# The opening of a transformer trunk as a stream by chunk: the first modulation computed slice by slice, its scale on TensorE and its shift on VectorE

## The reference

```python
cond = jax.nn.silu(c)
for i in range(DEPTH):
    mod = (cond @ mod_w[i] + mod_b[i])[:, None, :]
    shift1, scale1, gate1, shift2, scale2, gate2 = jnp.split(mod, 6, axis=-1)
    h = rms_norm(x, norm1_gain[i]) * (1 + scale1) + shift1
    y = swa_sink_attention(h, ...)          # layer 0; layer 1: gmlp_spatial_gating
    x = x + gate1 * y
    h = rms_norm(x, norm2_gain[i]) * (1 + scale2) + shift2
    x = x + gate2 * squared_relu_mlp(h, mlp_w1[i], mlp_w2[i])
```

## Time and profile before

| | |
|---|---|
| device time, median of 3 runs | 2563.44 us (2560.73 to 2566.36) |
| span of the profiled execution | 2568.1 us |
| TensorE busy in the span | 2438.0 us (95%) |
| VectorE busy | 1059.8 us (41%) |
| ScalarE busy | 650.8 us (25%) |
| GpSimd busy | 506.9 us (20%) |
| transfers | 189.01 MB, mean 74 GB/s |
| mean granted TensorE clock | 0.975 |

### The profile page before, as it was taken

How to read it: one execution, slowest core, us unless ns; L and a number is a source line. 1 busy time by engine, 2 the same in 40 slices (tenths; PEclk the granted TensorE clock), 3 DMA queues, 4 the chain that set the end, 5 groups by cost and what they waited for, 6 DMA issues and landing times.

```text
span 2568.1 us, 28722 instructions
## 1 busy us (share of the span) xinstructions
PE 2438.0 (95%) x10592; PEld 1942.8 (76%) x10592; DVE 1059.8 (41%) x1190; ACT 650.8 (25%) x719; POOL 506.9 (20%) x232
## 2 busy tenths in 40 slices
PE   3997889899999999998999999999899999999999
PEld 2776458688888888887788788788678888888887
DVE  7655965633333333334432442343522323232232
ACT  3322531321221221212322331122331221221221
POOL 1111221112212212211211112112122221222121
PEclk9887989899999999999999999999899999999999
DMA  6342131121221221221244221221011111111112
GB/s 240 107 140 68 37 150 41 64 84 49 75 80 49 83 72 52 87 66 41 98 127 143 89 74 41 73 82 49 25 49 50 49 41 50 49 47 43 49 49 82
DMA packets 70592, 189.01 MB, mean 74 GB/s; under 512 B 23440, under 2 KB 25360, under 8 KB 70032
## 3 DMA queue, kind: packets, MB, share of 16 engines
q1 hardware_dynamic: 52144, 127.64, 15.4%
q10 hardware_dynamic: 18400, 60.69, 6.8%
HBM read 170.48 MB, written 16.78 MB: 73 GB/s over the span
## 4 chain that ended last, share of the span: by engine, by line
issue 65%; PE 27%; POOL 7%; POOLq 0%; DVE 0%; ACT 0%; DVEq 0%
PE pp L1034 27%; POOL w_lo L267 7%; POOL pr L279 1%; POOLq L287 0%; POOLq L266 0%; DVE x L921 0%; POOLq L283 0%; DVE mod_t L624 0%; ACT tmp L307 0%; POOLq L273 0%; POOLq L278 0%; POOL kf L270 0%; POOLq L267 0%; POOL vt L271 0%; DVEq L921 0%
## 5 line engine op out<-in xcount | busy, mean ns | idle before, releaser
L267 POOL TENSOR_TENSOR w_lo<-w_raw,w_hi 128x1024 fp32r<-128x1024 f32 x194 | 473.2, 2439 | 1942.4 <-ACT w_hi L298 1942.4
L1034 PE MATMUL pp<-h_hi,w_hi 128*128 128x512 f32 x1824 | 605.7, 408 | 35.1 <-DVE h_lo L715 23.3
L1034 PE MATMUL pp<-h_lo,w_hi 128*128 128x512 f32 x1824 | 595.2, 402 | 0.0
L1034 PE MATMUL pp<-h_hi,w_lo 128*128 128x512 f32 x1824 | 593.7, 401 | 0.0
L298 ACT ACTIVATE w_hi<-w_raw 128x1024 fp32r<-128x1024 f32 x194 | 205.0, 1057 | 959.6 <-PE pp L1034 916.9
L1034 PEld LDWEIGHTS pp<-h_hi,w_hi 128*128 128x128 f32 x1824 | 346.6, 192 | 129.3 <-issue 22.4
L1034 PEld LDWEIGHTS pp<-h_lo,w_hi 128*128 128x128 f32 x1824 | 350.5, 192 | 85.3 <-issue 1.0
L1034 PEld LDWEIGHTS pp<-h_hi,w_lo 128*128 128x128 f32 x1824 | 349.6, 192 | 85.7
L1034 PE MATMUL pp<-hid_hi,w_hi 128*128 128x512 f32 x1280 | 410.4, 398 | 0.0
L1034 PE MATMUL pp<-hid_hi,w_lo 128*128 128x512 f32 x1280 | 409.0, 397 | 0.0
L1034 PE MATMUL pp<-hid_lo,w_hi 128*128 128x512 f32 x1280 | 408.9, 397 | 0.0
(11 more groups left out here) (133 smaller groups left out, 1225.0 us busy)
## 6 DMA issues: line engine op xcount, KB each, us to landing
w_raw<-weights SPq DMA_DIRECT2D x194, 512.0 KB, 3.3
mod_t<-mod_w ACTq DMA_DIRECT2D x64, 512.0 KB, 3.4
mod_first<-mod_w SPq DMA_DIRECT2D x16, 512.0 KB, 15.5
mod_late<-mod_w ACTq DMA_DIRECT2D x2, 4096.0 KB, 19.3
v_dram<-v_out ACTq DMA_DIRECT2D x16, 512.0 KB, 5.5
vf<-v_dram ACTq DMA_DIRECT2D x16, 512.0 KB, 4.4
x<-x_in SPq DMA_DIRECT2D x4, 1024.0 KB, 9.1
qf<-q_dram SPq DMA_DIRECT2D x32, 128.0 KB, 2.5
```

The source lines that it names most:

```text
L267: nc.gpsimd.tensor_tensor(out=w_lo[:, s, :, :], in0=w_raw[:, s, :, :], in1=w_hi[:, s, :, :].bitcast(f32), op=ALU.subtract).then_inc(lo_don ...
L1034: last = T.matmul(pp[s][:, cs], w[:, s, k, :], r[:, k, cs], start=(k == 0 and w is w_hi and r is hi), stop=(k == KC - 1 and w is w_lo))
```

## The change

The five small loads move from SP's queue to ScalarE's, so that x is the first thing SP loads, and the positions are staged in `sin` instead of `qa`. `mod_first` shrinks from sixteen whole tiles to four slots of 1 MB; a load now brings, for one output chunk k, the 128 outputs of both shift and scale from all eight input chunks. Slots are used again once both users are done with them.

The shift of chunk k is accumulated on VectorE in `shift_rows(k)`: eight operations of 128 x 128 in place of a share of eight operations of 128 x 1024. The scale of chunk k is eight matmuls on TensorE, with the weight block as the stationary operand and one column of `cond` moving; one more matmul sums the shift accumulator. VectorE adds bias and gain to one column at a time. h follows chunk by chunk, and the two units of the first pair follow h, with the modulation of chunk k+2 ahead of the products of chunk k on TensorE.

```diff
             for i in range(4):
                 sp.dma_start(x[:, 2 * i:2 * i + 2, :], x_in[:, 2 * i:2 * i + 2, :]).then_inc(x_ld[i], 16)
-            for q in range(2 * KC):
-                if q == KC:
+            for k in range(KC):
+                if k == 3:
                     for s in range(2):
                         sp.dma_start(w_raw[:, s, :, :], weights[s]).then_inc(raw_in[s], 16)
-                sp.dma_start(mod_first[:, q, :], mod_w[q]).then_inc(mf_in[q], 16)
+                if k >= 4:
+                    sp.wait_ge(sh_acc, k - 3)
+                    sp.wait_ge(gv_scale, k - 3)
+                sp.dma_start(mod_first[:, k % 4, :, :, :].rearrange("p a c f -> p (a c) f"),
+                             mod_w[0:2 * KC, :, P * k:P * k + P].rearrange("q p f -> p q f")).then_inc(mf_in[k % 4], 16)
...
+            act.dma_start(cond[:, 0, :], c_in).then_inc(c_ld, 16)
+            act.dma_start(colt[:, :], cols).then_inc(const_in, 16)
+            act.dma_start(ones[:, :], mats[:, 1, :]).then_inc(const_in, 16)
+            act.dma_start(ident[:, :], mats[:, 0, :]).then_inc(const_in, 16)
+            act.dma_start(sin[:, :].bitcast(i32), pos_in).then_inc(pos_s, 16)
...
+            def shift_rows(k):
+
+                dve.wait_ge(mf_in[k % 4], 16 * (k // 4) + 16)
+                acc = mod_acc[:, P * k:P * k + P]
+                own(V.tensor_scalar(acc, mod_first[:, k % 4, 0, 0, :], cond[:, 2, 0:1], None, ALU.mult))
+                for c in range(1, KC):
+                    ins = V.scalar_tensor_tensor(out=acc, in0=mod_first[:, k % 4, 0, c, :], scalar=cond[:, 2, c:c + 1],
+                                                 in1=acc, op0=ALU.mult, op1=ALU.add)
+                    if c < KC - 1:
+                        own(ins)
+                ins.then_inc(sh_acc, 1)
...
+                def modulation(k):
+                    place = HALF * (k % 2)
+                    dve.wait_ge(gv_scale, k + 1)
+                    dve.wait_ge(gv_shift, k + 1)
+                    V.tensor_scalar(mod[:, SHIFT1, k:k + 1], pp[3][:, place:place + 1], mod_b(SHIFT1)[:, k:k + 1], None,
+                                    ALU.add).then_inc(mf_used, 1)
+                    V.tensor_scalar(amp[:, 0, k:k + 1], pp[3][:, place + 1:place + 2], mod[:, SCALE1, k:k + 1],
+                                    ngain(0)[:, k:k + 1], ALU.add, ALU.mult).then_inc(mf_used, 1)
+                    dve.wait_ge(mf_used, 2 * k + 2)
...
+                for k in range(KC):
+                    modulation(k)
+                    if k == 0:
+                        dve.wait_ge(bc_done, 2)
+                    scaled(k)
+                    if k + 2 < KC:
+                        shift_rows(k + 2)
+                    if k:
+                        low(k - 1)
+                low(KC - 1)
...
+            shift_rows(0)
+            for half in range(2):
+                deviations(0, half)
+            shift_rows(1)
+            first_norm()
...
+            def modulation(k):
+
+                place = HALF * (k % 2)
+                pe.wait_ge(mf_in[k % 4], 16 * (k // 4) + 16)
+                if k >= 2:
+                    pe.wait_ge(mf_used, 2 * k - 2)
+                for c in range(KC):
+                    last = T.matmul(pp[3][:, place + 1:place + 2], mod_first[:, k % 4, 1, c, :], cond[:, 2, c:c + 1],
+                                    start=c == 0, stop=c == KC - 1)
+                last.then_inc(gv_scale, 1)
+                pe.wait_ge(sh_acc, k + 1)
+                T.matmul(pp[3][:, place:place + 1], mod_acc[:, P * k:P * k + P], ones[:, 0:1],
+                         start=True, stop=True).then_inc(gv_shift, 1)
+
+            def first_pair():
+
+                ready(0, 0)
+                ready(0, 1)
                 for k in range(KC + LAG):
                     if k < KC:
+                        if k + 2 < KC:
+                            modulation(k + 2)
                         pe.wait_ge(h_done, k + 1)
                         last = products(0, k, h_hi, h_lo)
...
             for half in range(2):
                 token_squares(0, half)
-            mod_columns(0, mf_used, KC)
+            pe.wait_ge(cond_done, 1)
+            modulation(0)
             for half in range(2):
                 spread_norm(0, half)
-            mod_columns(1, mf_used, 2 * KC, tmp[:, 0, :], 0)
+            modulation(1)
```

More of the change, by code:

```diff
@@ L77, in build @@
         sink8 = sb("sink8", [P, 2 * 4])
-        with ExitStack() as first:
-            mod_first = sb("mod_first", [P, 2 * KC, S], where=first)
         h_hi = sb("h_hi", [P, KC, S], f32r)
@@ L92, in build @@
                 sin = sb("sin", [P, S], f32, rope)
+                with ExitStack() as first:
+                    mod_first = sb("mod_first", [P, 4, 2, KC, P], f32, first)
                 qa = sb("qa", [P, 2, S], f32, rope)
@@ L141, in build @@
         x_ld = [sem(f"x_ld{i}") for i in range(4)]
-        mf_in = [sem(f"mf_in{i}") for i in range(2 * KC)]
-        pos_s = sem("pos_s")
+        mf_in = [sem(f"mf_in{i}") for i in range(4)]
+        sh_acc, gv_shift, gv_scale = sem("sh_acc"), sem("gv_shift"), sem("gv_scale")
+        pos_s, cond_done = sem("pos_s"), sem("cond_done")
         dv = sem("dv")
@@ L314, in deviations, with first_norm @@
                                      bias=eps, scale=1.0 / D).then_inc(sd_done, 1)
[L316 to L323, removed]
+            def first_norm():
+                for k in range(KC):
+                    act.wait_ge(t_done, k + 1)
+                    nc.scalar.activation(h_hi[:, k, :], tmp[:, k % 2, :], ACT.Identity,
+                                         bias=mod[:, SHIFT1, k:k + 1]).then_inc(nh_done, 1)
             def closing(pair, n):
@@ L343, in closing @@
                 split_hi(pair + 1, 0)
-                act.wait_ge(mod_done, 3 * n + 2)
+                act.wait_ge(mod_done, 3 * n)
                 for k in range(4):
@@ L373, in _ @@
             split_hi(0, 1)
-            norm(0)
+            first_norm()
             def head_roots(j, heads):
@@ L637, in mod_part @@
             def mod_part(part):
-                dve.wait_ge(mod_mm, part + 1)
+                dve.wait_ge(mod_mm, part - 1)
                 V.tensor_tensor(out=mod[:, bass.ds(part, 1), :].rearrange("p a k -> p (a k)"),
@@ L655, in gains @@
             def gains(n):
-                dve.wait_ge(mod_done, 3 * n + 2)
+                dve.wait_ge(mod_done, 3 * n)
                 own(V.scalar_tensor_tensor(out=amp[:, n, :], in0=mod[:, 3 * n + 1, :], scalar=1.0,
                                            in1=ngain(n), op0=ALU.add, op1=ALU.mult))
[L660 to L686, removed]
@@ new lines, in first_norm, with scaled, low @@
+            def first_norm():
+                def modulation(k):
[7 more added lines that the diff above has]
+                    dve.wait_ge(mf_used, 2 * k + 2)
+                def scaled(k):
+                    if k >= 2:
+                        dve.wait_ge(h_done, k - 1)
+                    V.scalar_tensor_tensor(out=tmp[:, k % 2, :], in0=x[:, k, :], scalar=amp[:, 0, k:k + 1],
+                                           in1=pp[2][:, :], op0=ALU.mult, op1=ALU.mult).then_inc(t_done, 1)
+                def low(k):
+                    dve.wait_ge(nh_done, k + 1)
+                    V.scalar_tensor_tensor(out=h_lo[:, k, :], in0=tmp[:, k % 2, :], scalar=mod[:, SHIFT1, k:k + 1],
+                                           in1=h_hi[:, k, :].bitcast(f32), op0=ALU.add, op1=ALU.subtract).then_inc(h_done, 1)
+                for k in range(KC):
+                    modulation(k)
[7 more added lines that the diff above has]
+                low(KC - 1)
@@ L755, in _ @@
             own(V.reciprocal(cond[:, 1, :], cond[:, 1, :]))
-            own(V.tensor_tensor(out=cond[:, 2, :], in0=cond[:, 0, :], in1=cond[:, 1, :], op=ALU.mult))
+            V.tensor_tensor(out=cond[:, 2, :], in0=cond[:, 0, :], in1=cond[:, 1, :], op=ALU.mult).then_inc(cond_done, 1)
+            dve.wait_ge(cond_done, 1)
             dve.wait_ge(const_in, 48)
             V.tensor_scalar(sink8[:, :], colt[:, sink0:sink0 + 2 * 4], 8.0, None, ALU.mult).then_inc(sink8_done, 1)
+            own(V.tensor_scalar(mod[:, SCALE1, :], mod_b(SCALE1), 1.0, None, ALU.add))
             dve.wait_ge(pos_s, 16)
-            own(V.tensor_copy(cos[:, :], qa[:, 0, :].bitcast(i32)))
+            own(V.tensor_copy(cos[:, :], sin[:, :].bitcast(i32)))
             for k in range(KC):
                 add_square(k, k % 2)
[L764 to L783, removed]
+            shift_rows(0)
+            for half in range(2):
+                deviations(0, half)
+            shift_rows(1)
+            first_norm()
             V.memset(mod_acc[:, :], 0.0).then_inc(acc_zero, 1)
@@ L1047, in unit @@
                 last.then_inc(gemm, 1)
-            def normed_pair(pair):
-                ready(pair, 0)
-                ready(pair, 1)
+            def modulation(k):
+                place = HALF * (k % 2)
```

(8 more changed lines are left out.)

5 lines of the change are left out of this document (removed).

## The result

The changed kernel takes 2577.92 us (median of 5 runs, 2572.02 to 2580.58); the kernel before, run beside it, 2565.9 us. The ratio is 1.0049, with a 95% interval from 1.0034 to 1.0064: slower by 12.6 us by that ratio (12.0 between the two medians), where 8.5 were forecast.

What follows compares the result with a forecast made beforehand. VectorE's chain to the last h_lo and 18.8 us beyond was taken to bound the opening; 12.7 us gained before the first product and 21.2 lost after gave 2563.4+8.5 = 2572 us, range 2559 to 2578.

Steps and rivals of the forecast that it cites:

- The path: Opening: the last h_lo counts, not the first product; 18.8 us of VectorE's own work follow up to the head sums.
- Loads: Opening: x issued 2.3 us earlier, squares end 1.8 us earlier, at 19.1 (17.7 to 20.9); small loads charged nothing.
- From the squares to the first product: Opening, after the squares' end at 19.1: first product at 42.8 instead of 55.46, with 2.0 us charged for GpSimd's w_lo.
- The stream: First product to last h_lo: 38.4 us instead of 17.2, so 21.2 lost.
- The mixed case: TensorE's clock in the stream partly slow, partly full: 7.3 us for each of two chunks; 2572 us, chance 0.45.
- The sum: At the last h_lo: 12.7 us gained up to the first product, 21.2 lost after; net +8.5, at 81.2.
- Nothing gives a delay back: Later steps: a delay of TensorE moves the waits along, so the end moves with the head sums, 91.4 to about 100.
- Slow chunk loads: Rival, opening: chunk loads take 7 us each, first h_lo at 50, +8 on top, 2580 us; chance 0.09.
- Cheap short operations: Rival, shift on VectorE: a slice costs 2.2 us; with full clock last h_lo at 69.8, 2559 us possible; chance 0.10.
- Full clock throughout: Rival, stream: TensorE holds 2.4 GHz from the first h on, last h_lo at 73.7, +1.0, 2564 us; chance 0.19.

Runs made afterwards that it cites:

- e1: The changed kernel with the five small loads back on SP's queue ahead of x; ratio 1.0025 against the kernel before.
- e2: The kernel before with only the five small loads moved to ScalarE's queue; ratio 1.0026 against the kernel before.
- f2: e1 with two of the eight scale matmuls for each chunk; 2567.44 us in one run (before 2565.39).
- f1: e1 with each shift slice cut to two of its eight operations; 2563.69 us in one run (before 2565.39).
- e4: The changed kernel with small loads first on SP's queue and contiguous chunk loads; ratio 1.0025 against the kernel before.
- j2: The changed kernel with x loaded in 16 pieces of 256 KB instead of 4 of 1 MB; 2568.69 us in one run (before 2560.55).
- e3: The changed kernel with chunk loads of one run of 8 KB a partition instead of sixteen of 512 B; ratio 1.0054 against the kernel before.
- h1: The kernel before with the positions loaded behind x and converted after the norm; ratio 0.9998 against the kernel before.
- g1: h1 with scale tiles first and the scale split, half on TensorE, half on VectorE in wide operations; ratio 0.9987 against the kernel before.

## Why the prediction was right in its sign and too small

*The path.* Right. What counts is the last h_lo, and 18.8 us of VectorE's own work follow; every kernel shows it. The first product came earlier and was worth nothing, as said.

*Loads: the step that failed.* "I let the squares end 1.8 us earlier, at 19.1 (bounds 17.7 and 20.9)" and "ScalarE now issues the five small loads ahead of its exponential; the conditioning is needed only after 19 us, so nothing is charged." They ended at 26.95, 7.8 us later and 6 us outside the bounds. The forecast counted 1.8 of the 2.3 us by which x is issued earlier as a gain, and put the small loads' delay beside another queue's 4 MB at nothing. The runs show that the small loads landed about one to each 1 MB piece of x, 2.8 us apart, and that VectorE's own order (constants, then the cast, then squares) put all five of them ahead of the squares. e1 and e2 size it from both sides: 7.9 us taken off the changed kernel at the head sums, 6.9 laid on the kernel before. No bound in the prediction covered it, since no row of before had two queues loading at once in the opening; the range held the time only just, and only because an error in the stream went the other way. That is luck.

*From the squares to the first product.* 23.7 us forecast, 22.7 measured (26.95 to 49.65). The spread matmuls ended 11.2 us behind the squares, forecast 11.3. GpSimd's w_lo fell on slice 1 and not on the slices behind the spread matmuls; it cost VectorE 4 us there, but as VectorE had to wait for the spread matmuls anyway, only 1.2 counted, where 2.0 were charged.

*The stream.* Forecast 38.4 us from the first product to the last h_lo, measured 34.6. The parts were right: a slice 2.85 against 2.99, VectorE's chunk 5.9 against 5.74 with TensorE relieved (f2), TensorE's 6.5 at 1.2 GHz against 6.40 (f1). The chunk loads, for which 3.5 us were taken between 2.6 and 7, ran at 290 GB/s, 3.6 us. What was too slow is the clock's share. Modulations 3 to 7 ended at 56.2, 62.6, 67.4, 75.1 and 79.9, 23.7 us in all, where 6.5, 6.5, 7.3 and 7.3 make 27.6. The rise came in the first burst of twelve products and one chunk before it the passes were fast already. The mixed case was the right one; in this execution it was mis-sized by 3.9 us.

*The sum.* Squares +7.8, start -1.0, stream -3.8 is +3.0 on the forecast 81.2, and the last h_lo was at 84.27. Without the loads' error the forecast would have been 4.8 us too long in this execution. The runs with early squares lie between that and no error: +3.7 at the head sums in e1, +5.8 in e4, +7.1 in j2, against the 8.5 forecast; by time e1 and e4 are both at +6.4.

*Nothing gives a delay back.* Right for the timed ratios: +11.6, +6.9, +15.1, +5.8, -0.4 and -4.2 at the head sums (changed, e2, e3, e4, h1, g1) became +12.6, +6.7, +13.9, +6.4, -0.5 and -3.3 us. In e1 +3.7 became +6.4, whose interval (3.6 to 9.2) still holds it. Between two single executions it doesn't hold: those traced lie only 2.1 us apart at the end, 9.5 less than at the head sums, by falls of the clock in either. That is why the parts of this study were sized by marks and not by spans.

*The other rivals.* Slow chunk loads: out, as e3 and e4 gained nothing and nothing waited for a chunk; a chunk took 3.6 us and not 7. Cheap short operations: out, 2.99 a slice against 2.2. Full clock throughout: out by the windows.

Open is how exactly the two queues take turns, by whole loads or otherwise: the landings at 16 pieces don't separate it from SP's pace of issuing. Open too is how much of the clock's course in the stream can be steered, which was not tried.

## What to carry to other kernels

Find out which engine's wait ends last after the stretch you speed up; an earlier first product is worth nothing while another engine's chain goes on behind it. A small load that many things wait for belongs in front of the large ones on the same queue; on a second queue it may wait for a whole large piece each time, so count landings there in pieces and not in bytes. And when work is cut to stream, look at what the cut does to the operation: eight 128-wide operations took 3.0 us where one 1024-wide one took 1.4 (9.62 us for seven), and the one-column passes on TensorE ran at the lower clock for most of the stream (3.4 us for sixteen instead of 1.8), so both engines needed more time than the earlier start had won.

## What the runs showed of the hardware that was not expected

A load of 4 KB on ScalarE's queue landed 5.2 us after its issue and one of 64 KB 12.0 us after it while SP loaded 4 MB; in front of x on SP's queue they took 1.8 and 1.9 (e1). Cutting x from 4 to 16 pieces brought the 64 KB load to 5.7 us. Loads of 2048 runs of 512 B ran at 290 GB/s, against some 415 GB/s in runs of 8 KB, and three of them held SP's queue for 15.93 us (11.38 in j2), where three in runs of 8 KB held it for 1.53 (e3). TensorE worked without a gap from 21 to 63 us in f1 and was at its lower level all that time.
